# State stage of an S5 layer on one Trainium2 core: input products by column tiles, six rows' joins added by TensorE, table slots moved, two low parts later, first chunk behind four rows

## The chip, the cores and the metric

One core of one Trainium2 chip runs the whole kernel as one program. The metric is device time in microseconds (us), the median of several runs. Engines are named as in the profile: PE is TensorE (PEld its weight loads), DVE is VectorE, ACT is ScalarE, POOL is GpSimd, and SP is the queue that issues most DMAs. Each engine works through its own list in order and waits on semaphores.

## The reference

Two layers of a decoder over 256 tokens of width 2048. Layer 0 is attention; layer 1 is an S5 state-space layer with a GLU. Each layer ends with a LayerNorm, a SwiGLU feed-forward and another LayerNorm. The change lies in layer 1, in `_s5_glu`:

```python
u = h.astype(f32).reshape(B, S, S5_GROUPS, S5_GROUP)          # 128 groups of 16 channels
bu = jnp.einsum('bsgc,gpc->bsgp', u.astype(jnp.complex64), B_bar)
_, states = lax.associative_scan(combine, (a, bu), axis=1)    # 64 complex states a group
y = jnp.einsum('bsgp,gcp->bsgc', states, C_mat).real.reshape(B, S, D)
y = y + d_skip.astype(f32) * h.astype(f32)
z = jax.nn.gelu(y).astype(h.dtype)
val, gate = jnp.split(z @ w_glu, 2, axis=-1)
return val * jax.nn.sigmoid(gate)
```

## The kernel before

Most of the time goes to weight products. A weight matrix comes in chunks of 512 KB (two row tiles of 128 by 512 columns) into a ring of four `RAW` slots. ACT rounds a chunk to its high part (`hi`, L835), DVE subtracts to get the low part (`lo`, L1193), and PE multiplies high by high, low by high and high by low (L406 to L408): 12 matmuls a chunk. `load` (L282) issues the next chunk when `lo` has let go of its slot; semaphore `lo_ready` counts low parts.

The state stage stands between the last chunk of layer 0 and the GLU product. It works on 16 rows of 128 channels; a row has 512 state values (4 pairs of groups, real and imaginary, 64 slots of 4 tokens each).

1. **Input products** (L760). For a row, 8 matmuls with a 128 by 128 table `TS` as weights and 64 columns of `U4` as moving data fill one PSUM bank. ACT copies the bank to `ST` (L1121, semaphore `e_out`).
2. **Joins** (`join`, L1923). DVE turns slots into pairs of slots: `product` (L1905, coefficient times odd slots, 496 elements), `total` (L1910) and the sum with the even slots into the chain buffer `CH` (L1932). Two rows are interleaved. After 8 rows `join_fours` (L1958 to L1962) goes on to fours; then come 8 more rows and a second `join_fours`.
3. **Chain** (`chain_op`, L2002 to L2008): 14 serial steps over both halves on DVE.
4. **Going back down**: `fill_fours` (4 rows at a time), ACT's `even_states` (L1128) copies the even slots from `CH` into `ST`, and `grow` (DVE: L1905, L1910, L1946) fills the odd slots of a row.
5. **Local products** (L772): PE multiplies `UT` by the table `KTAB` in 32 by 32 tiles, into the banks that the outputs use. It waits for all 16 `e_out`.
6. **Read-outs** (`read_out`, L784): for a row 32 matmuls with 32-column weights from the row's second table and 64 columns of `ST`; the innermost loop goes over four groups of 32 PSUM partitions. Then ACT takes the gelu (L1137) of two rows at a time and its high part (L1145), and DVE the low part (`split_z`, L2030). GLU chunk `j` (`first_chunk`) needs rows 2j and 2j+1. `add_zeros` (L801) puts matmuls with a zero operand between.

A trace record of an fp32 matmul in L760, L784, L772 or L801 comes twice per matmul. SP loads the tables (16 input tables L311, 16 output tables L315) into 14 slots of 4 KB per partition, each when its slot is free, and after them the GLU chunks 4 to 7. `CH` lies in the first 16 KB, where the `RAW` ring is: the four low parts of GLU chunks 0 to 3 are made before it is written. The hand-written order on PE is:

```python
for row in range(5):
    add_zeros((26, 0, 4, 0, 8)[row])
    read_out(row)
add_zeros(6)
for j in range(per):
    first_chunk(j)
    for row in range(2 * j + 5, 2 * j + 7 if j < 4 else 2 * j + 8 if j == 4 else 0):
        read_out(row)
```

POOL loads the gains `GB` after the last input product and the input of the next small product (`p_tok`, L2332) after the last read-out; PE turns it (L450) right after GLU chunk 7.

Of the kernel before, what the change touches and what calls it, by code (L numbers as in the profile page):

```python
# [25 lines left out]
P = 128  # L26
# [3 lines left out]
KT = D // P  # L30
# [52 lines left out]
def build(nc, t, out):  # L83
# [3 lines left out]
    with ExitStack() as ctx:  # L87
# [54 lines left out]
        slot_kb = [160, 164, 48, 64, 52, 68, 56, 72, 60, 76, 168, 172, 176, 180]  # L142
# [46 lines left out]

        def tile_of(row):  # L190

            return row // 2 + KT // 2 * (row % 2)
# [39 lines left out]
        e_done, e_out, square, joined, grown, even_out = sem("e_done"), sem("e_out"), sem("square"), sem("joined"), sem("grown"), sem("even_out")  # L232
        fours_joined, fours_filled = sem("fours_joined"), sem("fours_filled")
# [34 lines left out]
        def _(sp):  # L268
# [40 lines left out]
            def input_table(row):  # L309

                sp.dma_start(TS[row % 14][:], e_dram[tile_of(row)].rearrange("p (a c n) -> p a c n", a=4, c=2)).then_inc(ts_in[row % 14], 16)  # L311

            def output_table(row):

                sp.dma_start(TS[row % 14][:], c_dram[tile_of(row)].rearrange("p (a c n) -> p a c n", a=4, c=2)).then_inc(ts_in[row % 14], 16)  # L315
# [6 lines left out]
            def out_with_tables():  # L322

                nb, per, c0, _ = PHASES["outB0"]
                for j in range(nb * per):
# [5 lines left out]
                    if j >= 8 and j % 4 == 0:  # L331
                        input_table(j // 4)
# [5 lines left out]
            def s5_loads():  # L338
# [9 lines left out]
                for row in (0, 1, 10, 11, 12, 13):  # L348
                    input_table(row)
                for row in (14, 15):  # L350
                    sp.wait_ge(e_done, row - 13)
                    input_table(row)
                for row in range(2, 14):
                    sp.wait_ge(e_done, row + 1)
                    output_table(row)
                for row in (0, 1):
                    sp.wait_ge(e_done, row + 15)
                    output_table(row)
                for row in (14, 15):
                    sp.wait_ge(y_done, row - 13)  # L360
                    output_table(row)
                sp.wait_ge(even_out, KT)
                for j in range(RING):
                    sp.wait_ge(y_done, 2 * j + 6)
                    glu_chunks(RING + j, RING + j + 1)
# [31 lines left out]
        def _(pe):  # L397
# [349 lines left out]
            for row in range(KT):  # L747
                pe.wait_ge(ts_in[row % 14], 16 if row < 14 else 32)
# [1675 lines left out]
```

## Time and profile before

| | us |
|---|---|
| median of 3 runs (2291.73 to 2292.98) | 2292.68 |
| the profiled execution's own time | 2296.42 |
| its span (first to last instruction) | 2294.6 |
| PE busy in the span | 2266.1 (99%) |
| DVE busy | 1679.3 (73%) |
| ACT busy | 1033.2 (45%) |

The span is that of the instructions, the time that of the whole execution. PE is busy almost everywhere; the places where it is not are few, and a share of busy time hides them. The state stage (about 1192 to 1310 us from the span's start) is read from the timelines of its engines.

### The profile page before, as it was taken

What the parts mean: (1) busy time and instruction counts of PE and PEld (TensorE: products, weight loads), DVE (VectorE), ACT (ScalarE), POOL (GpSimd) and SP (SyncE); (2) the same over time, 40 slices, a digit from 0 to 9 for tenths busy, and PEclk for the clock granted to TensorE, in tenths of its full rate; (3) what the DMA queues carried; (4) which work ended last, traced back from release to release, by engine and by line L of the source; (5) the groups of instructions that cost most, each with busy time, mean ns of one, the idle gap of its engine ahead of it and who ended that gap; (6) DMA issues with size and microseconds to landing.
All of it is one profiled execution on the core that took longest, in us unless ns stands there. A gap on an engine that the chain in (4) does not pass through costs nothing.

```text
span 2294.6 us, 34806 instructions
## 1 busy us (share of the span) xinstructions
PE 2266.1 (99%) x12036; PEld 1883.5 (82%) x12036; DVE 1679.3 (73%) x2539; ACT 1033.2 (45%) x1162; POOL 223.3 (10%) x322
## 2 busy tenths in 40 slices
PE   9999999999999999999999999999999999999998
PEld 7888888888887888888878788888888888888886
DVE  5775758778888878788879756766777654577666
ACT  4445636444444334444342544544455433444442
POOL 1000069701111111000100000000000000000000
PEclk9999999999999999999999999999999999999999
DMA  7655365778786777666765456665655666656664
GB/s 255 197 190 176 107 225 175 216 251 269 260 272 225 256 244 237 221 223 220 266 238 187 143 192 194 216 224 194 197 192 186 199 194 194 195 188 193 198 192 138
DMA packets 134619, 478.51 MB, mean 209 GB/s; under 512 B 15968, under 2 KB 19296, under 8 KB 133360
## 3 DMA queue, kind: packets, MB, share of 16 engines
q1 hardware_dynamic: 120720, 427.87, 56.8%
q0 software_dynamic: 13648, 49.12, 6.7%
q8 instruction: 71, 1.16, 0.2%
q14 instruction: 36, 0.29, 0.0%
q10 hardware_dynamic: 144, 0.07, 0.0%
HBM read 457.85 MB, written 19.14 MB: 208 GB/s over the span
## 4 chain that ended last, share of the span: by engine, by line
PE 94%; DVE 4%; ACT 1%; issue 1%; DMA 1%; DVEq 0%; ACTq 0%; SPq 0%
PE ps L406 29%; PE ps L408 29%; PE ps L407 29%; PE ps L760 1%; PE ps L450 1%; PE ps L784 1%; PE ps L420 0%; PE ps L422 0%; PE ps L421 0%; DVE w_lo L1193 0%; DVE gated L1607 0%; PE ps L675 0%; DMA raw<-in_w_outA 0%; DVE gated L1905 0%; DVE scan_wide L1958 0%
## 5 line engine op out<-in xcount | busy, mean ns | idle before, releaser
L1193 DVE TENSOR_TENSOR w_lo<-raw,w_hi 128x1024 fp32r<-128x1024 f32 x771 | 945.8, 1232 | 510.0 <-ACT w_hi L835 502.9
L835 ACT ACTIVATE w_hi<-raw 128x1024 fp32r<-128x1024 f32 x771 | 813.5, 1059 | 986.7 <-PE ps L408 863.0
L406 PE MATMUL ps<-w_hi,x_hi 128*128 128x512 f32 x2304 | 901.2, 391 | 2.0 <-DVE x_lo L2030 1.8
L408 PE MATMUL ps<-w_hi,x_lo 128*128 128x512 f32 x2304 | 897.5, 390 | 0.0
L407 PE MATMUL ps<-w_lo,x_hi 128*128 128x512 f32 x2304 | 897.3, 389 | 0.0
L406 PEld LDWEIGHTS ps<-w_hi,x_hi 128*128 128x128 f32 x2304 | 432.8, 188 | 92.1 <-issue 2.2
L408 PEld LDWEIGHTS ps<-w_hi,x_lo 128*128 128x128 f32 x2304 | 432.9, 188 | 90.8
L407 PEld LDWEIGHTS ps<-w_lo,x_hi 128*128 128x128 f32 x2304 | 433.0, 188 | 88.9
L406 PE MATMUL ps<-w_hi,hid_hi 128*128 128x512 f32 x656 | 256.8, 392 | 1.3 <-DVE w_lo L1193 1.3
L407 PE MATMUL ps<-w_lo,hid_hi 128*128 128x512 f32 x656 | 255.5, 389 | 0.0
L408 PE MATMUL ps<-w_hi,hid_lo 128*128 128x512 f32 x656 | 255.3, 389 | 0.0
L1607 DVE STREAM_TRANSPOSE gated<-gated 32x128 f32<-32x128 f32 x704 | 213.0, 303 | 9.8
L406 PEld LDWEIGHTS ps<-w_hi,hid_hi 128*128 128x128 f32 x656 | 123.1, 188 | 30.3 <-DVE w_lo L1193 3.1
L408 PEld LDWEIGHTS ps<-w_hi,hid_lo 128*128 128x128 f32 x656 | 123.1, 188 | 25.8
L407 PEld LDWEIGHTS ps<-w_lo,hid_hi 128*128 128x128 f32 x656 | 123.1, 188 | 25.2
L2143 POOL TENSOR_TENSOR s_small<-s_small 64x128 f32<-64x128 f32 x93 | 81.9, 881 | 7.5
L1049 ACT ACTIVATE hid_hi<-gated 128x512 f32 (+1 forms) x44 | 27.9, 633 | 120.7 <-DVE gated L1607 120.7
L2264 POOL DMA_DIRECT2D s_e_dram<-s_e x16 | 8.9, 556 | 335.6 <-DVE s_e L1687 335.6
L2113 POOL DMA_DIRECT2D gb<-in_ln_g x4 | 2.2, 544 | 397.6 <-DVE res L2063 128.6
L2257 POOL DMA_DIRECT2D s_coef<-s_coef_dram x64 | 35.4, 559 | 4.7 <-DMA s_coef_dram<-s_small 4.5
L1592 DVE TENSOR_TENSOR gated<-ps,gated 128x512 f32<-128x512 f32 x44 | 30.1, 685 | 5.7 <-ACT gated L1044 5.6
L1615 DVE TENSOR_TENSOR hid_lo<-gated,hid_hi 128x512 f32 (+1 forms) x44 | 30.1, 684 | 0.0
(306 smaller groups left out, 1431.0 us busy)
## 6 DMA issues: line engine op xcount, KB each, us to landing
raw<-in_w_inA SPq DMA_DIRECT2D x192, 512.0 KB, 4.2
raw<-in_w_inB SPq DMA_DIRECT2D x160, 512.0 KB, 4.2
raw<-in_w_outA SPq DMA_DIRECT2D x96, 512.0 KB, 4.2
raw<-in_w_outB SPq DMA_DIRECT2D x80, 512.0 KB, 4.2
raw<-in_w_in SPq DMA_DIRECT2D x64, 512.0 KB, 4.4
raw<-in_w_gate SPq DMA_DIRECT2D x64, 512.0 KB, 3.7
raw<-in_w_glu SPq DMA_DIRECT2D x64, 512.0 KB, 4.2
raw<-in_w_out SPq DMA_DIRECT2D x32, 512.0 KB, 3.4
```

Source lines behind the costliest of these rows:

```text
L406: pe.matmul(o, hi[:, kt + k, cols], WH[:, s, k, 0:width], start=(kt + k == 0), stop=False)
L407: pe.matmul(o, hi[:, kt + k, cols], WL[:, s, k, 0:width], start=False, stop=False)
L408: last = pe.matmul(o, lo[:, kt + k, cols], WH[:, s, k, 0:width], start=False, stop=(kt + k == depth - 1))
L450: last = pe.transpose(TP[:, g % 2, k, q * P:(q + 1) * P], src[:, q, col + k * P:col + (k + 1) * P], ID[:])
L835: act.activation(WH[:, s, :, 0:width], RAW[:, s, :, 0:width], ACT.Copy).then_inc(hi_ready, 1)
L1049: act.activation(HH[:, bass.ds(lin(2 * k, 2 * coef, i), 2), :], GT[:, 0], ACT.Copy).then_inc(hid_hi, 1)
L1193: dve.tensor_tensor(WL[:, s, :, 0:width], RAW[:, s, :, 0:width], WH[:, s, :, 0:width].bitcast(F32), ALU.subtract).then_inc(lo_ready, 1)
L1592: dve.tensor_tensor(GT[:, 1], A[:, bb % 2, :, 256:512], GT[:, 0], ALU.mult).then_inc(hid_ready, 1)
L1607: last = dve.transpose(turned_of[32 * j:32 * j + 32, :, :, r, :], rows_of[32 * r:32 * r + 32, :, :, j, :])
L1615: dve.tensor_tensor(HL[:, rows, :], GT[:, 0], HH[:, rows, :].bitcast(F32), ALU.subtract).then_inc(hid_split, 1)
L2143: link(pool.tensor_tensor(o, a, b, op))
L2257: pool.dma_start(EC[n][PW * s:PW * (s + 1)].rearrange("p a c n -> p a (c n)"), src).then_inc(e_raw[n], 16)
```

## The change

- **Input products.** Each matmul of 128-column weights is split into four with 32-column weights, one per group of 32 PSUM partitions, with the same moving data. `U4` is laid out with the row first.
- **Joins of rows 8 to 13.** DVE makes the product alone, into a buffer of the row's own (`SPREAD`). PE adds both its halves to the even slots of the row's PSUM bank, with the identity as weights (4 matmuls a row, 124 columns each, PSUM step 2), and ACT copies the even slots to `CH`. Rows 14 and 15 are joined as before, after the six products. Local products and the second `join_fours` wait for all six copies (`chain_out`).
- **Tables.** Rows 0 to 7 are loaded early (before: rows 2 to 9), and rows 14 and 15 take the slots of rows 8 and 9, behind five output tables.
- **Low parts.** Only those of GLU chunks 1 and 2 are made before the joins. The one of chunk 0 comes after the second `grow` pair, that of chunk 3 after the fifth. `CH` moves off their `RAW` slots, so chunk 4 can be loaded after `lo` of chunk 0, chunks 5 and 6 after 8 `even_states`, and chunk 7 after `lo` of chunk 3.
- **End of the stage.** PE reads out four rows, then does chunk 0, and from there two rows behind each of chunks 0 to 5. ACT takes gelu 0 and 1 ahead of the even states of rows 4 to 7. POOL's `GB` load waits for all even states.

```diff
-        CH = [at(f"chain{h}", [P, SLOTS // 2, PAIRS], 8 - 8 * h) for h in range(2)]
-        U4 = at("u_by_pair", [P, 4, KT, SLOTS], 96)
+        CH = [at(f"chain{h}", [P, SLOTS // 2, PAIRS], kb) for h, kb in enumerate((0, 100))]
+        U4 = at("u_by_pair", [P, KT, 4, SLOTS], 96)
+        SPREAD = [at(f"spread{n}", [P, 2, 2, 4, SLOTS // 2 - 1], kb) for n, kb in enumerate((96, 98, 202, 204, 108, 110))]
...
-                        last = pe.matmul(PS[:, row % 8, o:o + SLOTS], TS[row % 14][:, a, ri, :], U4[:, a, row, :], start=True, stop=True)
+                        for n_ in range(4):
+                            cols = slice(PW * n_, PW * (n_ + 1))
+                            last = pe.matmul(PS[cols, row % 8, o:o + SLOTS], TS[slot_of(row)][:, a, ri, cols], U4[:, row, a, :], start=True, stop=True)
                 last.then_inc(e_done, 1)
+            for row in range(8, 14):
+                pe.wait_ge(spread, row - 7)
+                for o in range(2):
+                    even = PS[:, row % 8, 4 * SLOTS * o:4 * SLOTS * (o + 1)].rearrange("p (a n) -> p a n", n=SLOTS)[:, :, 2:SLOTS:2]
+                    for c in range(2):
+                        last = pe.matmul(even, ID[:], SPREAD[row - 8][:, o, c], start=False, stop=(c == 1), skip_group_check=True)
+                last.then_inc(added, 1)
...
             pe.wait_ge(e_out, KT)
+            pe.wait_ge(chain_out, 6)
...
-            for row in range(5):
-                add_zeros((26, 0, 4, 0, 8)[row])
+            add_zeros(24)
+            for row in range(4):
                 read_out(row)
-            add_zeros(6)
+            add_zeros(10)
             for j in range(per):
                 first_chunk(j)
-                for row in range(2 * j + 5, 2 * j + 7 if j < 4 else 2 * j + 8 if j == 4 else 0):
-                    read_out(row)
+                if j < 6:
+                    read_out(2 * j + 4)
+                    read_out(2 * j + 5)
...
+            for row in range(8, 14):
+                act.wait_ge(added, row - 7)
+                first = 8 * (row % 8)
+                act.activation(CH[row // 8][:, 1:SLOTS // 2, first:first + 8].rearrange("p m x -> p x m"),
+                               PS[:, row % 8, :].rearrange("p (x n) -> p x n", n=SLOTS)[:, :, 2:SLOTS:2], ACT.Copy).then_inc(chain_out, 1)
...
-            for j in range(RING):
-                lo(PHASES["glu"][2] + j)
+            lo(PHASES["glu"][2] + 1)
+            lo(PHASES["glu"][2] + 2)
...
+            for row in range(8, 14):
+                dve.wait_ge(e_out, row + 1)
+                if row == 12:
+                    dve.wait_ge(e_done, KT)
+                product(row, slots_of(row, 1), SPREAD[row - 8]).then_inc(spread, 1)
+            for n_ in range(3):
+                join(14, n_)
+                join(15, n_)
+            dve.wait_ge(joined, 30)
+            dve.wait_ge(chain_out, 6)
+            join_fours(1)
...
-            pool.wait_ge(e_done, KT)
+            pool.wait_ge(even_out, KT)
             load_gb(1)
```

The first place is DVE's list at the second half of the joins: `spread` is a row's product for PE, `gated` the buffer of the usual join, `chain_93` the second half of `CH`. Before:

```order
L1962 TENSOR_TENSOR chain_92<-chain_92,scan_wide_115 128x15x8x4
L1905 TENSOR_TENSOR gated<-a_bar,states 128x496 x2
L1910 TENSOR_TENSOR gated<-gated 128x2x124 x2
L1932 TENSOR_TENSOR chain_93<-gated,states 128x8x31 x2
...
L1958 TENSOR_TENSOR scan_wide_114<-a_bar_111,chain_93 128x960
```

and now:

```order
L1998 TENSOR_TENSOR chain_92<-chain_92,scan_wide_121 128x15x8x4
L1941 TENSOR_TENSOR spread_95<-a_bar,states 128x496
...
L1941 TENSOR_TENSOR spread_100<-a_bar,states 128x496
L1941 TENSOR_TENSOR gated<-a_bar,states 128x496 x2
L1946 TENSOR_TENSOR gated<-gated 128x2x124 x2
L1968 TENSOR_TENSOR chain_93<-gated,states 128x8x31 x2
L1994 TENSOR_TENSOR scan_wide_120<-a_bar_117,chain_93 128x960
```

Four groups of six instructions became six single products and one such group.

The second place is PE's list from the last input product to the local products. Before:

```order
L760 MATMUL ps<-u_by_pair,s_table_97 128x64 x8
L760 MATMUL ps<-u_by_pair,s_table_98 128x64 x8
L772 MATMUL ps<-u,s_k 32x256 x4
```

and now:

```order
L773 MATMUL ps<-u_by_pair,s_table_111 32x64 x32
L773 MATMUL ps<-u_by_pair,s_table_112 32x64 x32
L780 MATMUL ps<-spread_95,ident 128x4x31 x4
...
L780 MATMUL ps<-spread_100,ident 128x4x31 x4
L793 MATMUL ps<-u,s_k 32x256 x4
```

A row has 32 matmuls in place of 8, and 24 additions that wait for DVE stand ahead of the local products.

The third place is DVE's list after the first `fill_fours`, where the low parts (`w_lo`, `x_lo`) stand between the rows, now:

```order
L1982 TENSOR_TENSOR states<-states,gated 128x8x31 x2
L1994 TENSOR_TENSOR scan_wide_120<-a_bar_117,chain_92 128x15x32
...
L1998 TENSOR_TENSOR chain_92<-chain_92,scan_wide_121 128x15x4x4
L2075 TENSOR_TENSOR x_lo<-z,x_hi 128x512
L1229 TENSOR_TENSOR w_lo<-raw,w_hi 128x1024
L1941 TENSOR_TENSOR gated<-a_bar,states 128x496 x2
```

Before, no low part of z and none of a weight stood between the second and the third pair of rows.

## Rows read from the trace of the kernel before
**Rows 1.** The page's first line: the whole execution.
```profile
span 2294.6 us, 34806 instructions
```
**Rows 2.** Busy time by stretch: length, PE, PEld, DVE, ACT, POOL; then PE's clock, DMA share, GB/s.
```profile
1231.30:1249.40 18.10, 17.79 (x513) 15.05 (x513) 18.03 (x78) 1.46 (x2) 0.73 (x2) 1.00 0.46 175
1255.40:1258.30 2.90, 0.01 (x1) 0.00 (x1) 2.32 (x6) 2.12 (x4) 0.00 (x0) 0.75 0.00 0
1258.30:1267.10 8.80, 8.77 (x260) 8.51 (x264) 5.23 (x13) 2.34 (x4) 0.00 (x0) 0.50 0.41 123
1273.90:1277.30 3.40, 3.40 (x10) 2.65 (x9) 3.37 (x10) 0.00 (x0) 0.00 (x0) 0.50 0.00 0
```
**Rows 3.** Timeline of PE: start us, us, line, operation, count, [idle before].
```profile
1196.20 1.86 PE L733 MATMUL ps<-ident,res 128*128 128x128 f32 x15 [0.20 <-DVE res L1459]
...
1201.83 28.80 PE L760 MATMUL ps<-u_by_pair,s_table 128*128 128x64 f32 x256
1231.31 7.69 PE L772 MATMUL ps<-u,s_k 32*32 32x256 f32 x215 [0.69 <-ACT states L1121]
...
1249.39 6.02 PE L801 MATMUL ps<-zeros,ident 128*128 128x64 f32 x52
1258.33 3.64 PE L784 MATMUL ps<-states,s_table 128*32 128x64 f32 x128 [2.92 <-DVE states L1946]
1261.90 1.97 PE L801 MATMUL ps<-zeros,ident 128*128 128x64 f32 x8
...
1277.72 1.99 PE L784 MATMUL ps<-states,s_table 128*32 128x64 f32 x128
...
1301.95 0.50 PE L406 MATMUL ps<-w_hi,x_hi 128*128 128x512 f32 x1
...
1310.26 0.60 PE L450 MATMUL ps<-ident,p_tok 128*128 128x128 f32 x4
```
**Rows 4.** Timeline of DVE, same columns.
```profile
1203.20 4.62 DVE L1193 TENSOR_TENSOR w_lo<-raw,w_hi 128x1024 fp32r<-128x1024 f32 x4
...
1217.07 0.68 DVE L1905 TENSOR_TENSOR gated<-a_bar,states 128x496 f32<-128x496 f32 x1 [0.48 <-ACT states L1121]
...
1219.37 2.23 DVE L1958 TENSOR_TENSOR scan_wide<-a_bar,chain 128x960 f32<-128x960 f32 x2
...
1223.90 1.26 DVE L1905 TENSOR_TENSOR gated<-a_bar,states 128x496 f32<-128x496 f32 x2
...
1234.82 2.23 DVE L1958 TENSOR_TENSOR scan_wide<-a_bar,chain 128x960 f32<-128x960 f32 x2
...
1239.36 0.49 DVE L2002 TENSOR_TENSOR scan_work<-a_bar,chain 128x128 f32<-128x128 f32 x2
...
1252.79 1.23 DVE L1958 TENSOR_TENSOR scan_wide<-a_bar,chain 128x480 f32<-128x480 f32 x2
...
1255.98 1.26 DVE L1905 TENSOR_TENSOR gated<-a_bar,states 128x496 f32<-128x496 f32 x2 [0.69 <-ACT states L1128]
...
1261.07 1.23 DVE L1958 TENSOR_TENSOR scan_wide<-a_bar,chain 128x480 f32<-128x480 f32 x2
...
1267.13 1.26 DVE L1905 TENSOR_TENSOR gated<-a_bar,states 128x496 f32<-128x496 f32 x2 [3.57 <-ACT states L1128]
```
**Rows 5.** Timeline of ACT, same columns.
```profile
1203.86 0.60 ACT L1121 ACTIVATE states<-ps 128x512 f32<-128x512 f32 x1 [0.73 <-PE ps L760]
...
1255.33 2.20 ACT L1128 ACTIVATE states<-chain 128x248 f32<-128x248 f32 x4 [22.55 <-DVE chain L1962]
...
1291.57 1.06 ACT L835 ACTIVATE w_hi<-raw 128x1024 fp32r<-128x1024 f32 x1 [3.80 <-DMA raw<-in_w_glu]
```
**Rows 6.** Instructions of the tile p_tok, with the time from issue to landing.
```profile
L2332 POOL DMA_DIRECT2D p_tok<-in_p x1: 734/734/734, 1302.3 to 1302.3; - x1
...
DMA to landing us min/median/max: 5.5/5.9/6.3
```
**Rows 7.** The same of the tables.
```profile
DMA to landing us min/median/max: 3.6/4.9/9.2
```

More of the change, by code:

```diff
@@ L188, in build, with slot_of @@
         c_dram = nc.dram_tensor("s5_c_dram", (KT, P, 4 * 2 * P), F32, kind="Internal").ap()
+        def slot_of(row):
+            return row if row < 14 else row - 6
         def tile_of(row):
@@ L747, in _ @@
             for row in range(KT):
-                pe.wait_ge(ts_in[row % 14], 16 if row < 14 else 32)
+                pe.wait_ge(ts_in[slot_of(row)], 16 if row < 14 else 32)
                 if row == 0:
@@ L776, in read_out @@
             def read_out(row):
-                pe.wait_ge(ts_in[row % 14], 32 if 2 <= row < 14 else 48 if row < 2 else 64)
+                pe.wait_ge(ts_in[slot_of(row)], 32 if row < 14 and row not in (8, 9) else 48 if row < 14 else 64)
                 pe.wait_ge(grown, 6 * (row // 2) + 5 + row % 2)
@@ L783, in read_out @@
                         for a in range(4):
-                            last = pe.matmul(outputs(row, a, s, s + 1), TS[row % 14][:, a, ri, PW * s:PW * (s + 1)],
+                            last = pe.matmul(outputs(row, a, s, s + 1), TS[slot_of(row)][:, a, ri, PW * s:PW * (s + 1)],
                                              ST[:, row, ri, a, :], start=False, stop=(ri == 1), skip_group_check=True)
@@ L1921, in join @@
             def join(row, n_):
-                done = 6 * (row // 2) + 2 * n_ + row % 2
+                done = 6 * (row // 2 if row < 8 else 4) + 2 * n_ + row % 2
                 if done >= 2:
@@ L1927, in join @@
                     dve.wait_ge(e_out, row + 1)
-                    ins = product(row, slots_of(row, 1))
+                    ins = product(row, slots_of(row, 1), wide[row % 2])
                 elif n_ == 1:
@@ L1941, in grow @@
                     dve.wait_ge(even_out, row + 1)
-                    ins = product(row, slots_of(row, 2))
+                    ins = product(row, slots_of(row, 2), wide[row % 2])
                 elif n_ == 1:
@@ L1980, in fill_fours @@
                         carry(4 * q, 4, n_, o, 2, 3).then_inc(fours_filled, 1)
-            dve.wait_ge(lo_ready, PHASES["glu"][2] + RING)
+            dve.wait_ge(lo_ready, PHASES["glu"][2] + 2)
             dve.wait_ge(square, 14)
-            for row in range(0, KT, 2):
+            for row in (0, 2, 4, 6):
                 for n_ in range(3):
@@ L1987, in _ @@
                     join(row + 1, n_)
-                if row % 8 == 6:
-                    dve.wait_ge(joined, 3 * (row + 2))
-                    join_fours(row // 8)
-                    dve.wait_ge(fours_joined, 6 * (row // 8 + 1))
+            dve.wait_ge(joined, 24)
+            join_fours(0)
+            dve.wait_ge(fours_joined, 6)
+            for row in range(8, 14):
+                dve.wait_ge(e_out, row + 1)
[8 more added lines that the diff above has]
+            join_fours(1)
+            dve.wait_ge(fours_joined, 12)
             def chain_op(h, n_, k):
@@ L2031, in split_z @@
                                   XH[:, rows, :].bitcast(F32).rearrange("p k n -> p (k n)"), ALU.subtract).then_inc(z_split, 1)
-            first = PHASES["glu"][2] + RING
+            first = PHASES["glu"][2]
             fill_fours(0)
-            for b in range(8):
+            grow_pair(0)
+            for b in range(1, 8):
                 grow_pair(b)
-                if b in (1, 2, 3):
+                if b > 1:
+                    split_z(b - 1)
+                if b < 4:
                     dve.wait_ge(grown, 6 * (b + 1))
@@ L2040, in _ @@
                     dve.wait_ge(fours_filled, 6 * (b + 1))
-                if 2 <= b < 6:
-                    split_z(b - 2)
-                if b == 6:
+                else:
+                    lo(first + b - 1)
+                if b == 1:
+                    split_z(0)
                     lo(first)
-                    split_z(4)
-            for b in range(5, 8):
-                lo(first + b - 4)
-                split_z(b)
+            lo(first + 7)
+            split_z(7)
             c0, b0 = PHASES["glu"][2:]
```

69 lines of the change are left out of this document (40 added, 29 removed).

## The prediction

> **What bounds the kernel now.** The span is 2294.6 us [rows 1], and outside the state stage PE runs without gaps, so only what moves the end of GLU chunk 7 moves the end of the kernel. I read the timelines of PE, DVE and ACT side by side through that stage, then the granted clock by stretch. From 1203.20 to about 1258 DVE has no gap to speak of: four low parts, the joins of rows 0 to 7 from 1207.85, `join_fours` at 1219.37, the second half's joins at 1223.90, `join_fours` at 1234.82, the chain at 1239.36, `fill_fours` at 1252.79, the first `grow` at 1255.98 [rows 4]. PE is behind it only once: row 7 comes 0.48 us late [rows 4]. PE's own work there (input products to 1230.6, local products from 1231.31 to 1249.39, zeros to 1255.4) ends early, and PE idles 2.92 us before the first read-out at 1258.33 [rows 3]. So the input products are not the bound, DVE's chain is.
>
> From 1258.33 the two alternate. In the idle time PE's clock falls from 2.4 to 1.2 GHz: mean 0.75 in that gap, 0.50 for the 8.8 us after it, and 0.50 again for 3.4 us under chunk 0 [rows 2]. At half clock two read-outs take 3.64 us against 1.99 at full [rows 3]. DVE waits 3.57 us at 1267.13 for even states that ACT holds back behind a high part and that behind a third read-out [rows 4], and ACT waits 3.80 us for a GLU chunk at 1291.57 [rows 5], since all chunk loads came after the last even state. Chunk 7 ends at 1310.26, where PE turns `p_tok` [rows 3].
>
> **Part 1, up to the second `join_fours`.** Two low parts less before the joins: 4.65 us for four [rows 4], so 2.33 less. The input products take 28.80 us for 16 rows, 1.79 each [rows 3]. The new ones have the form of a read-out (32 matmuls, 128 by 32 weights, 64 columns, four column groups innermost), which costs 0.96 us a row at full clock (1.99 us for two less the drain of the last) [rows 3]. So rows come at 0.96 us from 1201.83 and end near 1217.3. ACT's copy of 0.60 us [rows 5] keeps up, and row 7's wait (0.48) goes. Tables 14 and 15 are issued when rows 8 and 9 are done (1210.5 and 1211.5) behind five output tables. With a landing of 3.6 to 9.2 us [rows 7] row 15 may be up to 4.5 us late. Nothing needs it before DVE's fifth product at 1223.5, so I cost this at nothing.
>
> DVE then starts the joins at 1205.55, and the first `join_fours` ends 11.04 + 4.53 us later (from rows 4: 1219.37 less 1207.85 less 0.48, and 1223.90 less 1219.37), at T = 1221.1. Six products at 0.59 and one pair of joins (10.92 / 4 = 2.7) bring DVE to T + 6.3. PE cannot begin adding before the first product, at T + 0.7 = 1221.8. An addition is two records of a 128-wide identity; such a record costs 0.116 us with 64 zero columns (6.02 us for 52) and 0.12 in the token transposes (1.86 for 15) [rows 3]. Eight records a row are 0.9 us, six rows 5.4. But PE has then idled since about 1217.3, some 4.5 us, longer than the 2.92 us after which its clock stood at half [rows 2, 3]. The same record costs 0.24 at half clock (1.97 for 8) [rows 3], 1.8 us a row. Bounds for the end of the additions: 1227.2 at full clock, 1232.6 if all are at half. The half-clock stretches lasted 3.4 us under full chunks and 10.2 us from the gap on [rows 2], and the additions are dense, so I take a return after two to three rows, and an end at 1229.8. ACT's last copy and the hand-over add 0.9: J = 1230.7 (1228.2 to 1233.5) for the second `join_fours`, which stood at 1234.82. **Gain 4.1 us** (1.3 to 6.6).
>
> One rule speaks against this step. The identity's output has a PSUM step of two elements. The token transposes of L733 write with a far larger step (rearranged to `p q n s`) and cost 0.12 us a record, like the contiguous ones [rows 3]; I therefore charge nothing for the step. The Trainium skill (PSUM — Partial Sum Buffer, Specifications) says of PSUM that "any non-contiguous AP slows matmuls significantly". By that rule, with an estimate of twice the time, the sum would be 4 to 8 us less; it is rival C.
>
> **Part 2, chain and cover.** From `join_fours` to the first `grow` nothing changes: 1255.98 less 1234.82 = 21.16 us [rows 4], so `grow` starts at D = J + 21.2 = 1251.9 and row 0 can be read at D + 2.35 (1258.33 less 1255.98). PE's local products lose their head start: they too begin at J. They take 18.1 us and 24 zeros 5.5, so PE arrives at J + 23.6, and row 0 is ready at J + 23.5. The cover is used up to the last tenth, at no price, and the 2.92 us gap with its fall of the clock goes. What costs PE time after J now moves the end one for one.
>
> **Part 3, read-outs and chunks.** Times from D, with durations of [rows 3 to 5]: a pair of `grow` 2.55 (1261.07 less 1255.98, halved), `fill_fours` 2.54 (1255.33 less 1252.79), `split_z` 0.65, a low part 1.2, gelu 1.1, high part 0.55, two even states 1.1, a chunk 2.75 (8.31 us from 1301.95 to 1310.26 for three), two read-outs 1.92.
> - Rows 0, 1 from 2.35, rows 2, 3 from 4.9, zeros (2.3) to 9.1. DVE: `grow` 0 and 1, `fill_fours` 1 to 7.6, `split_z` 0 to 8.3, low part of chunk 0 to 9.5. Chunk 0 runs from 9.6 to 12.35. Even state 4 is there at 8.7 (gelu 1 starts at 7.0), so DVE no longer waits: the 3.57 us are gone, 1.85 of them refilled by the low parts.
> - Then DVE and PE keep step. `grow` 2 ends at 12.0, 3 at 17.7, 4 at 23.4, 5 at 27.7, 6 at 32.0, 7 at 36.3; chunks start at 14.3, 19.5, 25.3, 29.9, 34.6, 39.2 and 42.0. PE is short of work by 0.6, 1.0 and 0.2 us before rows 6, rows 8 and chunk 3.
> - Chunk 4 is issued at 9.6 and chunks 5 and 6 at 11, long before their high parts at 18, 24 and 27. Chunk 7 is issued at 25.4, needed at 31.7. The 3.80 us wait is gone.
> - Chunk 7 ends at D + 44.7. Before it was 1310.26 less 1255.98 = 54.3. **Gain 9.6 us.**
>
> New at the end: `p_tok` is issued after row 15, and now two chunks stand behind that row instead of three. Issue at D + 39.6 and 5.5 to 6.3 us to land [rows 6] give 45.1 to 45.9, against 44.7 for PE; the low part of chunk 8, behind `split_z` 7 and two norm steps of 1.2 us, ends at 45.3. **Loss 0.7 us.** `GB` now starts near D + 24 and is needed at D + 41.7: nothing. A clock that falls once more somewhere in part 3 costs half of a 3.4 us stretch, 1.7 us; PE has gaps of 1 us as the one before chunk 0, so I take 60% of it: **loss 1.0 us.**
>
> **Sum:** 4.1 + 9.6 − 0.7 − 1.0 = 12.0 us. Against the profiled execution (2296.42 us, a span of 2294.6 with 1.8 around it) that is 2284.4. The median of the runs is 3.74 lower, so I forecast 2292.68 − 12.0 = 2280.7 us.
>
> **Rivals.** No change means within 0.2% (4.6 us), about what a measurement of this kernel tells.
> - A, the clock never falls: J = 1228.2 and no loss in part 3, 2.5 + 1.0 more gain, 2277.2. For it: the local products hold 1.00 [rows 2]. Against it: 4.5 us without any matmul. Chance 0.12.
> - B, colder: additions all at half clock (2.8 later) and two more low stretches of 1.7, 2286.9. The 8.8 us at 0.50 under 32-column read-outs [rows 2] speak for it, as the stage is now richer in them. Chance 0.15.
> - C, strided additions twice as dear, by the rule above: J at 1234.7 to 1239, 4 to 8 us of the gain lost, 2284.7 to 2289. The row of L733 speaks against it. Chance 0.06.
> - D, the change doesn't do what it says: column tiles save nothing on the input products. They end at 1230.6, the additions at 1236.1, J = 1237.0, 6.3 later: 2287.0. The read-outs' 0.96 us speak against it. Chance 0.06.
> - E, slower: PE stays at half clock from the additions through the local products. These stood under the scan with 6 us of idle and zeros after them and now have no slack. Additions to 1232.6, J at 1233.5, 36.2 us of local products and 11 of zeros: row 0 at 1280.7 instead of 1254.3, 2280.7 + 26.4 = 2307. It decides once the low stretch eats 12 us, that is lasts some 24 us. I have no row of a rise under 32 by 32 tiles, only 1.00 throughout [rows 2]; but dense work raised the clock within 10.2 us. Chance 0.04.
>
> **Numbers.** The forecast has 0.57. The range reaches from A with a little more (2276.5) to B and the milder half of C and D (2287.5). Faster by over 0.2% (below 2288.1): forecast, A, nearly all of B and D, half of C, 0.88. Slower: E and a remainder, 0.05. Same: 0.07.
>
> **What would show it.** Input products at 0.96 us a row; DVE without a gap up to `join_fours`, then up to 4 us of waiting for ACT's last chain copy; additions at 0.9 or 1.8 us a row with the clock; row 0 with no gap before it and at full clock; chunk 0 9.6 us after the first `grow`; ACT never waiting for a GLU chunk; a wait of under 1 us at `p_tok`. Wrong if additions exceed 1.8 us a row, if the local products run at 0.50, or if chunk 7 ends later than 47 us after the first `grow`.

## The result and the profile after

The change makes the kernel **slower**: a median of 2301.68 us (2300.12 to 2303.34, 6 runs) against 2293.06 (2291.73 to 2294.49, 6 runs) before, a ratio of 1.0034 with a 95% interval of 1.0024 to 1.0044. The forecast was 2280.7, in a range of 2276.5 to 2287.5.

| | before | after |
|---|---|---|
| the profiled execution, us | 2296.42 | 2300.45 |
| its span | 2294.6 | 2298.7 |
| first input product | 1201.83 | 1201.72 |
| second `join_fours` (J) | 1234.82 | 1243.57 |
| first `grow` (D) | 1255.98 | 1264.74 |
| `p_tok` turned, behind GLU chunk 7 | 1310.26 | 1314.16 |
| from there to the end of the span | 984.3 | 984.5 |

In the two profiled executions all of the loss, and more, stands ahead of J: 8.75 us later, where 4.1 us earlier was forecast. Part 3 gives 4.9 back, against an execution of the kernel before that lies 3.4 us above its median. The timeline of PE after (columns as in [rows 3]) shows where it starts:

```profile
1201.72 1.53 PE L773 MATMUL ps<-u_by_pair,s_table 128*32 128x64 f32 x92
1204.13 1.99 PE L773 MATMUL ps<-u_by_pair,s_table 128*32 128x64 f32 x128 [0.88 <-issue]
1208.96 2.77 PE L773 MATMUL ps<-u_by_pair,s_table 128*32 128x64 f32 x127 [2.83 <-issue]
1212.96 3.64 PE L773 MATMUL ps<-u_by_pair,s_table 128*32 128x64 f32 x128 [1.23 <-issue]
1217.23 1.99 PE L773 MATMUL ps<-u_by_pair,s_table 128*32 128x64 f32 x127 [0.64 <-issue]
1221.07 1.99 PE L773 MATMUL ps<-u_by_pair,s_table 128*32 128x64 f32 x127 [1.84 <-issue]
1225.18 1.99 PE L773 MATMUL ps<-u_by_pair,s_table 128*32 128x64 f32 x127 [2.13 <-issue]
1232.60 4.71 PE L773 MATMUL ps<-u_by_pair,s_table 128*32 128x64 f32 x168 [5.43 <-issue]
1237.24 5.62 PE L780 MATMUL ps<-spread,ident 128*128 128x124 f32 x48
1243.62 17.59 PE L793 MATMUL ps<-u,s_k 32*32 32x256 f32 x512 [0.76 <-ACT chain L1149]
1261.14 5.57 PE L823 MATMUL ps<-zeros,ident 128*128 128x64 f32 x48
1267.09 1.99 PE L805 MATMUL ps<-states,s_table 128*32 128x64 f32 x128 [0.38 <-issue]
```

The products themselves run as forecast: 128 records, two rows, in 1.99 us. But after each 127 or 128 records PE stands idle, and the profile names "issue": it waited for no semaphore, no table, no engine. 128 matmul records with their 128 weight loads are 256 instructions. The DMA view of 1190 to 1245 us has a queue of kind "instruction" (packets, MB, share of 16 engines), before:

```profile
q8 instruction: 6, 0.10, 0.8%
```

and after:

```profile
q8 instruction: 9, 0.15, 1.1%
```

Packets of some 16 KB, three more of them in this window. Over the input products alone the same view counts 2 packets before (1201.7 to 1231.4) and 8 after (1201.7 to 1237.3). That is 512 and 2048 instructions in blocks of 256, and the whole span has 71 and 77. **PE's instructions are themselves loaded, 256 at a time, and the stretch now eats a block in 2 us while a new one comes every 4.2** (1204.13 to 1225.18 in five blocks). The Trainium skill (Runtime: NRT & Kernel Launch, Instruction fetch mechanics) describes such a refill in 16 KiB blocks of 256 instructions, and says that the cost of crossing a boundary is "mostly hidden"; the trace agrees with the block and not with the hiding. The longest gap, 5.43 us, stands behind 856 records, inside row 13, so it is not a wait for the tables of rows 14 and 15. DVE's waits in that time (timeline) are the consequence:

```profile
1210.46 0.68 DVE L1941 TENSOR_TENSOR gated<-a_bar,states 128x496 f32<-128x496 f32 x1 [1.64 <-ACT states L1144]
1214.99 0.68 DVE L1941 TENSOR_TENSOR gated<-a_bar,states 128x496 f32<-128x496 f32 x1 [1.78 <-ACT states L1144]
1218.73 0.68 DVE L1941 TENSOR_TENSOR gated<-a_bar,states 128x496 f32<-128x496 f32 x1 [0.99 <-ACT states L1144]
1237.43 1.26 DVE L1941 TENSOR_TENSOR spread<-a_bar,states 128x496 f32<-128x496 f32 x2 [9.43 <-PE ps L773]
1243.57 2.23 DVE L1994 TENSOR_TENSOR scan_wide<-a_bar,chain 128x960 f32<-128x960 f32 x2 [2.10 <-issue]
```

The last row but one are the products of rows 12 and 13, whose buffers lie on the part of `U4` that the last input products read: they wait 9.43 us for the last input product. By stretch (columns as in [rows 2]):

```profile
1201.70:1210.00 8.30, 4.59 (x304) 4.25 (x296) 6.88 (x11) 3.00 (x6) 0.00 (x0) 1.00 0.65 192
1210.00:1215.00 5.00, 3.77 (x147) 3.54 (x140) 2.76 (x7) 1.55 (x3) 0.00 (x0) 0.50 0.72 220
1237.20:1243.00 5.80, 5.66 (x53) 5.43 (x48) 4.03 (x8) 3.74 (x7) 0.00 (x0) 0.99 0.57 175
1243.00:1261.00 18.00, 17.38 (x512) 15.02 (x512) 17.40 (x88) 1.97 (x3) 0.00 (x0) 1.00 0.02 4
1264.00:1314.00 50.00, 44.97 (x1165) 37.46 (x1164) 42.80 (x84) 30.10 (x40) 1.84 (x3) 1.00 0.42 155
```

The clock stood at 0.50 from 1210 to 1215, after a stretch in which PE was idle for 3.7 of 8.3 us, and again under the last 168 products (4.71 us), after the gap of 5.43. It was at 1.00 under the local products and, as a mean, in all of part 3.

### The profile page after: what moved, and what is told of

Read it like the earlier page. It is cut to its first block, busy times and chain, and to the rows that moved or that the text cites. A ratio compares the mean times of both kernels' runs of the same rounds, so it can differ in the third digit from the quotient of the medians.

```text
span 2298.7 us, 36386 instructions
## 1 busy us (share of the span) xinstructions
PE 2255.7 (98%) x12832; PEld 1873.3 (81%) x12832; DVE 1674.2 (73%) x2527; ACT 1036.3 (45%) x1168; POOL 222.8 (10%) x322
## 4 chain that ended last, share of the span: by engine, by line
PE 94%; DVE 3%; issue 2%; DMA 1%; ACT 0%; POOL 0%; DVEq 0%; ACTq 0%; SPq 0%
PE ps L417 29%; PE ps L418 29%; PE ps L419 29%; PE ps L773 1%; PE ps L793 1%; PE ps L805 1%; PE ps L461 1%; DVE gated L1643 1%; DVE w_lo L1229 1%; PE ps L433 0%; PE ps L432 0%; PE ps L431 0%; DMA s_c_dram<-s_c_pow 0%; PE ps L823 0%; PE ps L686 0%
## 5 line engine op out<-in xcount | busy, mean ns | idle before, releaser
L773 PE MATMUL ps<-u_by_pair,s_table 128*32 128x64 f32 x1024 | 20.6, 252 | 15.0 <-issue 15.0
L1628 DVE TENSOR_TENSOR gated<-ps,gated 128x512 f32<-128x512 f32 x44 | 30.2, 686 | 4.6 <-ACT gated L1067 4.3
```

Source lines behind the costliest of these rows:

```text
L773: last = pe.matmul(PS[cols, row % 8, o:o + SLOTS], TS[slot_of(row)][:, a, ri, cols], U4[:, row, a, :], start=True, stop=True)
L1628: dve.tensor_tensor(GT[:, 1], A[:, bb % 2, :, 256:512], GT[:, 0], ALU.mult).then_inc(hid_ready, 1)
```

## The experiments

Theory F: the number of PE instructions, not their work, sets the end of the input products. F1 is its floor, a block at a time even on idle queues; F2 is contention, a block that comes late behind table transfers. J is given from the first input product, since that stood anywhere between 1200.3 and 1204.2 us from run to run; in the kernel before it is 33.0 us, after the change 41.9. Each ratio is against the kernel before, on the same chip. Medians of two runs can come from two chips, and then the ratios are the better comparison.

### Wide input products in the changed kernel

```diff
-                        for n_ in range(4):
-                            cols = slice(PW * n_, PW * (n_ + 1))
-                            last = pe.matmul(PS[cols, row % 8, o:o + SLOTS], TS[slot_of(row)][:, a, ri, cols], ...)
+                        last = pe.matmul(PS[:, row % 8, o:o + SLOTS], TS[slot_of(row)][:, a, ri, :], ...)
```

> Input products back to 8 matmuls of 128-wide weights a row, the rest as changed. Theory F (PE's instruction blocks of 16 KB come too slowly for 32 matmuls a row: the rows of the changed kernel show a gap after every 127 or 128 records): a row takes 1.79 us again without gaps, input products end at 1230.6, additions at about 1236.1, second join_fours at 1237.0 instead of 1243.6, so 6.5 us less than the changed kernel, near 2295. Rival T (tables 14 and 15 come late, the 5.43 us gap at 1227.2 is a wait for them): the gap stays, join_fours at 1240 or later, 0 to 3 us less. Rival K (the fall of PE's clock is what costs): no more than 2 us less.

Measured: 2294.34 us, ratio 1.0002 (0.9992 to 1.0012): 7.3 us less than the changed kernel, and no difference from the kernel before. PE's timeline has no gap:

```profile
1204.21 28.80 PE L771 MATMUL ps<-u_by_pair,s_table 128*128 128x64 f32 x256
1232.84 5.57 PE L778 MATMUL ps<-spread,ident 128*128 128x124 f32 x48
```

J is at 34.9 us (1239.12). The late tables were held to be worth 3 us at most and the clock 2, so neither explains it. It is the column tiles that made the change slower. The rest of it, with wide products, is worth nothing in the median.

### Column tiles alone in the kernel before

```diff
-                        last = pe.matmul(PS[:, row % 8, o:o + SLOTS], TS[row % 14][:, a, ri, :], ...)
+                        for n_ in range(4):
+                            cols = slice(PW * n_, PW * (n_ + 1))
+                            last = pe.matmul(PS[cols, row % 8, o:o + SLOTS], TS[row % 14][:, a, ri, cols], ...)
```

> The kernel before with nothing changed but the input products by 32-column tiles. Theory F: gaps after every 128 records, products end near 1232 to 1237 as in the changed kernel, joins of rows 12 to 15 wait for them; slower than before by 2 to 8 us. If column tiles did what the prediction took them to do (0.96 us a row) it is 0.5 us faster than before.

Measured: 2296.75 us, ratio 1.0016 (1.0006 to 1.0026). The same gaps stand between the blocks, 0.61, 2.83, 1.51, 1.19, 2.12, 2.40 and 1.14 us, and the products end near 1234.0. So the gaps don't need the rest of the change. J is at 35.6 us (1237.07), 2.7 later than before, where the changed kernel had it at 41.9: there the additions stand behind the late products. This profiled execution (2294.1) lies 2.7 us under the median of its runs. In it PE reached row 0 with a gap of only 0.28 us and kept its clock at 1.00 from there to the turn of `p_tok`, which was thus 1.8 us sooner behind the first input product than in the trace of before. So it doesn't show where the median loses its 3 us.

### Output tables out of the way

```diff
-                for row in range(5):
-                    sp.wait_ge(e_done, row + 1)
-                    output_table(row)
                 for row in (14, 15):
                     sp.wait_ge(e_done, row - 5)
                     input_table(row)
+                sp.wait_ge(e_done, KT)
+                for row in range(5):
+                    sp.wait_ge(e_done, row + 1)
+                    output_table(row)
```

> The changed kernel with the output tables issued only after the last input product; input tables 14 and 15 as before. It tells two forms of theory F apart. F1 (blocks have a floor of about 3.8 us each even with idle DMA queues, since the next one is asked for only when the last is begun): input products still take about 30 us and end near 1231. F2 (blocks are late because table loads fill the DMA queues): gaps shrink to under 0.5 us, input products end near 1219 to 1221, second join_fours near 1229 to 1231 and the kernel is 12 us faster than the changed one, near 2290. Rival T: input products end near 1219 too, but with the only gap before row 14.

Measured: 2298.6 us, ratio 1.0022 (1.0011 to 1.0032). PE's timeline is now regular:

```profile
1205.52 1.99 PE L774 MATMUL ps<-u_by_pair,s_table 128*32 128x64 f32 x128 [1.92 <-issue]
1208.98 1.99 PE L774 MATMUL ps<-u_by_pair,s_table 128*32 128x64 f32 x127 [1.46 <-issue]
...
1224.10 1.99 PE L774 MATMUL ps<-u_by_pair,s_table 128*32 128x64 f32 x127 [2.12 <-issue]
1227.95 1.99 PE L774 MATMUL ps<-u_by_pair,s_table 128*32 128x64 f32 x127 [1.86 <-issue]
...
1232.51 5.62 PE L781 MATMUL ps<-spread,ident 128*128 128x124 f32 x48
```

From 1205.52 to 1227.95 six blocks take 3.74 us each as a mean, on queues that are all but empty in the first of these stretches:

```profile
1204.00:1215.00 11.00, 5.97 (x383) 5.50 (x384) 8.79 (x17) 3.58 (x6) 0.00 (x0) 1.00 0.02 5
1215.00:1233.00 18.00, 9.15 (x553) 8.41 (x553) 11.46 (x21) 5.14 (x9) 0.00 (x0) 1.00 0.21 63
```

Blocks at a DMA share of 0.02 or less took 3.46 to 3.86 us, and two at 0.28 and 0.62 took 3.83 and 4.11. That is the floor of F1; the reason that F1 gives for it was not tested. F2 is what the output tables add: the products end 30.4 us after the first one instead of 35.5, and the gap of 5.43 is gone. J is at 36.8 us (1238.85) instead of 41.9. Of the 20 us between the forecast end of the products (1217.3) and the measured one, some 15 are the floor and some 5 contention, with the half clock that followed the long gap. The transfers that were moved then fell on the local products, whose blocks came late by 0.53 and 1.65 us.

### Two 64-column tiles instead of four of 32

```diff
-                        for n_ in range(4):
-                            cols = slice(PW * n_, PW * (n_ + 1))
+                        for n_ in range(2):
+                            cols = slice(2 * PW * n_, 2 * PW * (n_ + 1))
```

> The changed kernel with two 64-column tiles instead of four of 32: 16 matmuls a row, half the instructions of the changed kernel, twice those of before. Theory F with a block every 3.8 to 4.3 us: 64 instructions a row, a block lasts 4 rows, so 1.0 to 1.1 us a row; input products end near 1219, additions start as DVE gives them, join_fours near 1229 to 1231, 12 us faster than the changed kernel, near 2290. If narrow tiles were slow in themselves: no better than 1.79 us a row. Rival T: a gap of some 5 us before row 14 stays.

Measured: 2287.67 us, ratio 0.9975 (0.9965 to 0.9984): **faster than the kernel before**. PE's timeline:

```profile
1200.47 6.63 PE L773 MATMUL ps<-u_by_pair,s_table 128*64 128x64 f32 x219
1208.24 3.95 PE L773 MATMUL ps<-u_by_pair,s_table 128*64 128x64 f32 x127 [1.14 <-issue]
1213.33 3.94 PE L773 MATMUL ps<-u_by_pair,s_table 128*64 128x64 f32 x126 [1.14 <-issue]
1220.06 1.99 PE L773 MATMUL ps<-u_by_pair,s_table 128*64 128x64 f32 x40 [2.79 <-issue]
1221.98 6.58 PE L780 MATMUL ps<-spread,ident 128*128 128x124 f32 x48
```

A row costs 32 records of 0.031 us, 0.99 us, as much as 64 records of 0.0155 us with four tiles. The second halving saves nothing on PE and doubles the instructions. A block lasts 3.95 us here, just over the floor of 3.46 to 3.86. J is at 28.8 us (1229.27).

### Without PE's additions, wide and with half tiles

```diff
-            for row in range(8, 14):
-                pe.wait_ge(spread, row - 7)
...
-                product(row, slots_of(row, 1), SPREAD[row - 8]).then_inc(spread, 1)
...
+            for row in (8, 10, 12, 14):
+                for n_ in range(3):
+                    join(row, n_)
+                    join(row + 1, n_)
```

> The changed kernel with the input products back at 128 columns and without TensorE's additions: rows 8 to 15 are joined by DVE as before. What is left of the change is the low parts, the slots of the tables and the new order of read-outs, chunks and transfers. Theory F (only the number of PE instructions went against the change): J is set by the 28.8 us of wide products plus the last pair of joins, some 2.7 us sooner against the start of the products than with wide products and additions (34.9 us there), so about 32.2 us; the end is 2.7 us before that run, 2291.5. Rival (the additions do help even with wide products): not faster than 2294.3.

> 64-column tiles, and rows 8 to 15 joined by DVE instead of six of them added on PE. DVE alone sets the second join_fours: joins of the first half 11.0, join_fours 4.5, joins of the second half 10.9 from 1204.24 give J = 1230.7 against 1229.27 with the additions, so 1.4 us later, 2289.1. If the additions are worth what the prediction held, which had DVE out of work for up to 4 us, it is 4 us later (2291.5); if PE's extra 96 records and the instruction block that they need cost more than they give, it is faster than 2287.7.

Measured: 2294.22 us for the wide one, ratio 0.9999 (0.9990 to 1.0008), and 2291.8 with half tiles, 0.9989 (0.9980 to 0.9998). J came at 33.0 us (1234.47) and 30.2 us (1231.19), 1.9 us before and 1.4 us behind the runs with additions. The first should have gained 2.7 us against the run with additions and gained nothing; the second should have lost 1.4 and lost 4.1 by the medians, 3.2 by the ratios. Neither theory had the cause. Without additions the local products start early again and PE is idle ahead of row 0, for 3.95 and 7.70 us. With half tiles (PE's timeline, then the two stretches):

```profile
1254.70 6.07 PE L797 MATMUL ps<-states,s_table 128*32 128x64 f32 x256 [7.70 <-DVE states L1969]
```

```profile
1247.00:1254.70 7.70, 0.00 (x1) 0.04 (x2) 6.90 (x26) 2.20 (x4) 0.00 (x0) 0.65 0.00 0
1254.70:1260.70 6.00, 6.00 (x257) 5.91 (x257) 5.60 (x14) 1.77 (x2) 0.00 (x0) 0.60 0.02 5
```

Four rows take 6.07 us at a clock of 0.60, against 5.04 with two block gaps in the run with half tiles and additions (1252.77 to 1257.81). From row 0 to the turn of `p_tok` 50.3 and 50.0 us pass, against 48.0 and 46.6 with additions. So a part of what the additions give seems to be that they hold back PE's cover until it ends beside row 0. It is not the whole of it: both runs without additions also have a longer gap in the read-out of rows 10 and 11 (3.27 and 2.60 us, "issue"), with clocks of 0.85 and 0.72 beside it. No run divides the two.

### Fewer zeros

```diff
-            add_zeros(24)
+            add_zeros(12)
```

> 64-column tiles and 12 zeros instead of 24 behind the local products, nothing else. PE reaches the read-outs 2.8 us before row 0. If the idle time costs the clock, as before the change, where 2.92 us without work were followed by 8.8 us at 0.50, the first four rows take twice as long and the kernel is 1.5 to 3 us slower than with half tiles alone (2289 to 2291). If it doesn't, the time stays at 2287.7, and the zeros are not needed.

Measured: 2289.59 us, ratio 0.9981 (0.9972 to 0.9990), 1.9 us more than half tiles alone, on another chip; the intervals of the two ratios overlap. PE idles 3.03 us ahead of row 0, and four rows again take 6.07 us, as expected of the clock. Row 0 to the turn of `p_tok` is 49.0 us, 2.4 more than in the profile of half tiles alone. Four slow rows took 1 us more than there; behind them stands a second fall of the clock (0.66 in the stretch from 15 to 20 us behind row 0). Between the two this run doesn't divide the loss.

### GB later

```diff
             pool.wait_ge(even_out, KT)
+            pool.wait_ge(hi_ready, PHASES["glu"][2] + RING + 4)
             load_gb(1)
```

> 64-column tiles, and the two transfers of GB are issued only after the high part of GLU chunk 7 (some 10 us later). Theory G (GB takes the bandwidth that chunk 7 and the last tables need, and this reaches PE): ACT's wait of 5.2 us for chunk 7 falls under 2 us, PE's gaps between chunk 5 and chunk 6 (0.47 and 0.49) shrink, and the kernel is up to 1 us faster, 2286.7. Rival (PE has work all the time, so that wait costs nothing): ACT's wait shrinks and the turn of p_tok stands no earlier against row 0; GB, issued near 1287 and 8 to 12 us in landing, is then late for the norm at 1295.8, and the kernel is the same to 2 us slower.

Measured: 2288.47 us, ratio 0.9975 (0.9966 to 0.9984), as without this edit. ACT's wait for chunk 7 (5.05 us in the changed kernel, 5.21 with half tiles) is gone altogether; in its place DVE waits 1.44 us for `GB` and PE 1.02 us for `p_tok`. The rival is borne out in the time: the kernel is no faster. That the wait itself cost nothing isn't shown, since the later `GB` brought PE's wait of 1.02 us with it.

### Four rows added instead of six

```diff
-            for row in range(8, 14):
+            for row in range(8, 12):
                 pe.wait_ge(spread, row - 7)
...
+            for row in (12, 14):
+                for n_ in range(3):
+                    join(row, n_)
+                    join(row + 1, n_)
```

> 64-column tiles, and only rows 8 to 11 added by PE; DVE joins rows 12 to 15, which fills the 3.07 us that it waited for the additions. If the rest of that wait is PE's (products until 1222.0, six rows of additions 6.6): four rows end near 1226.4 and DVE's own work at 1219.8 + 2.4 + 5.4 = 1227.6, J 1.6 us earlier, 2286.0. If what limits J is something else (the last copy of ACT, the landing of tables 14 and 15), J stays at 1229.3 and the time at 2287.7.

Measured: 2287.64 us, ratio 0.9969 (0.9958 to 0.9981), J at 28.6 us (1229.35) where 1.6 us less than 28.8 was expected. PE's timeline says why:

```profile
1220.89 2.40 PE L773 MATMUL ps<-u_by_pair,s_table 128*64 128x64 f32 x40 [3.89 <-issue]
1223.22 5.42 PE L780 MATMUL ps<-spread,ident 128*128 128x124 f32 x32
```

The last block of products came 3.89 us late, and the additions behind it cost 0.17 us a record at a clock of 0.69, where with six rows they cost 0.14 at 0.85. Two rows less on PE were eaten by that.

### Half tiles with quiet tables, with six and with four rows

Output tables after the last input product and 12 zeros, in the kernel with half tiles; the second has four rows added as well.

> 64-column tiles, the output tables issued only after the last input product, and 12 zeros instead of 24 behind the local products (2.8 us less, as room for gaps there). Theory F2 (the long gap of 2.8 to 3.9 us before the last block of the input products is an instruction block that comes late because table transfers fill the DMA queues): that gap falls to 1.5 us or less, the products end 1.5 to 2.5 us sooner, J is at most 27.5 us after the first product instead of 28.8, and the kernel is 1 us faster than with half tiles alone, 2286.5. If a block takes its time with idle queues too, or if the moved transfers then hold up the blocks of the local products by more than the 2.8 us of room, it is at 2287.7 or later.

> 64-column tiles, four rows added by PE and four joined by DVE, the output tables after the last input product, 12 zeros. With the late block out of the way PE ends four rows of additions near 25 us after the first product, and DVE's own work (27.1 us after it) sets J: 1.7 us before half tiles alone, 2286.0, if theory F2 of the run with quiet tables holds. If J follows the blocks all the same, J stays at 28.5 us after the first product and the time at 2287.6.

Measured: 2286.73 us, ratio 0.9970 (0.9957 to 0.9982), and 2286.94, 0.9974 (0.9964 to 0.9983). The gap before the last block shrinks to 1.73 and 0.80 us, and with idle queues up to 472 records run without a gap. PE's timeline with six rows:

```profile
1205.41 11.30 PE L774 MATMUL ps<-u_by_pair,s_table 128*64 128x64 f32 x380 [0.56 <-issue]
1218.44 1.91 PE L774 MATMUL ps<-u_by_pair,s_table 128*64 128x64 f32 x40 [1.73 <-issue]
1222.04 7.78 PE L781 MATMUL ps<-spread,ident 128*128 128x124 f32 x48 [1.69 <-DVE spread L1942]
```

The products end 18.4 us after the first instead of 21.5, but J stays at 28.6: PE is now early, waits 1.69 us for DVE, and its additions take 7.78 us at a clock of 0.71. F2 holds for the gap; of the 3.1 us that the products gained, half is left when DVE's product is there, and the rest is given back at the lower clock. The first read-outs were cold here as well: after 1.65 us without work 256 records took 5.44 us at 0.70. With four rows PE waits 3.89 us for DVE and 32 additions take 6.42 us at 0.57. DVE's own work then sets J, at 27.2 us (1227.46) as expected, but row 0 to the turn of `p_tok` took 48.9 us instead of 46.6.

### The same with 19 zeros

> 64-column tiles, four rows added by PE, the output tables after the last input product, and 19 zeros, which reach to row 0 within 0.5 us where 12 left PE idle for 1.96 us. If that idle time is what made part 3 of the run with 12 zeros 2.3 us longer (row 0 to the turn of p_tok 48.9 us, against 46.6 with half tiles alone), it is 46.6 us again, and with J at 27.2 us after the first product the kernel comes to 2285.3. If part 3 stays at 48 to 49 us, the loss comes from the instruction blocks and tables around chunk 0, and the time stays at 2286.9.

Measured: **2285.55 us**, ratio 0.9966 (0.9954 to 0.9979). PE's timeline:

```profile
1249.89 4.46 PE L824 MATMUL ps<-zeros,ident 128*128 128x64 f32 x38
1254.59 1.99 PE L806 MATMUL ps<-states,s_table 128*32 128x64 f32 x128 [0.24 <-issue]
...
1301.58 0.66 PE L462 MATMUL ps<-ident,p_tok 128*128 128x128 f32 x4
```

J is at 27.2 us again, and row 0 to `p_tok` is 47.0 us, near the 46.6 expected. That seems to bear out the idle time as the cause, but the stretches say otherwise. With 12 zeros:

```profile
1260.97:1265.97 5.00, 2.87 (x132) 2.23 (x130) 4.97 (x13) 0.00 (x0) 0.00 (x0) 1.00 0.61 214
1265.97:1270.97 5.00, 5.00 (x49) 3.79 (x48) 3.46 (x9) 4.84 (x7) 0.00 (x0) 0.66 0.01 3
```

Its first four rows ran at full clock behind the 1.96 us of idle time. What it lost it lost 15 us behind row 0, after the gap of 2.13 us in the read-out of rows 4 and 5. All runs with this order and additions have such a gap; the fall after it only some:

| run | row 0 to `p_tok`, us | gap in rows 4 and 5 | clock 15 to 20 us behind row 0 |
|---|---|---|---|
| changed kernel | 47.1 | 1.74 | 1.00 |
| half tiles | 46.6 | 2.23 | 1.00 |
| wide inputs | 48.0 | 2.00 | 0.66 |
| half, GB later | 48.0 (1.02 of it `p_tok`) | 2.28 | 0.66 |
| half, 12 zeros | 49.0 | 2.58 | 0.66 |
| four tiles, quiet | 47.7 (0.50 of it `p_tok`) | 2.44 | 1.00 |
| half, four rows added | 47.1 | 1.20 | 1.00 |
| half, quiet, 12 zeros | 46.7 | 1.28 | 1.00 |
| half, four, quiet, 12 zeros | 48.9 | 2.13 | 0.66 |
| half, four, quiet, 19 zeros | 47.0 | 2.30 | 1.00 |

After a gap of 2.0 to 2.6 us there the clock fell in four profiles of seven. Those four took 48.0 to 49.0 us (one of them with 1.02 of waiting for `p_tok`), and all others 46.6 to 47.7. Half tiles with quiet tables and 12 zeros had slow first rows and no fall there, and took 46.7: so slow first rows alone need not cost anything. Whether the zeros ahead of row 0 have a part in the later fall is open; it was not tried apart from them. This version has the lowest median of all. Its interval overlaps that of half tiles alone, so that it beats those is not shown; that both beat the kernel before is.

## Why the prediction was wrong

- **The step that failed** is in part 1: "So rows come at 0.96 us from 1201.83 and end near 1217.3." The price of a row was right where PE ran. What failed was to carry a price read from 128 records over to 1024 in a row, with nothing in the sum for the supply of the instructions themselves. The products ended at 1237.3, 20 us later. In the trace of before, 32-column tiles only come in stretches of up to 256 records, between chunks (12 records in 2.75 us) and zeros, or at half clock, where a block lasts 3.64 us [rows 3]; a new block had time to arrive. The sign was there all the same, in PE's timeline of that trace: `1300.80 1.23 PE L784 MATMUL ps<-states,s_table 128*32 128x64 f32 x71 [0.73 <-issue]`. Over 8 blocks in a row the floor is about 3.7 us a block. 2048 instructions took 30.4 us even without the output tables beside them, more than the 28.80 of the wide products.
- **Rival D** (the column tiles save nothing) came nearest in its place, with 0.06, but it held 2287.0, since it let the products end at 1230.6 and the additions go well. They ended 6.7 us later than that, some 5 of them contention, and J came 6.6 us after its 1237.0. Against the profiled execution 3 us more are those of part 3, which the rival took from the forecast. The rival on the slower side (E, half clock under the local products) did not happen: 1.00 there.
- **Additions**: 48 records in 5.62 us at full clock, 0.117 each, as forecast at the lower bound. I had put them at half clock for two to three rows after 4.5 us without work; there was no such pause, because the products were late. The half tiles with quiet tables made one, and there the fear came true: after waits of 1.69, 3.89 and 3.21 us a record of the additions cost 0.16, 0.20 and 0.17 us, at clocks of 0.71, 0.57 and 0.69. The PSUM step of two costs nothing here, with 124 columns; rival C fell. (A record of zeros with 64 columns takes as long, 0.116, so the columns are not what sets the time, and a dearer write could hide behind it.) The rule of the Trainium skill behind it (PSUM — Partial Sum Buffer, Specifications: "any non-contiguous AP slows matmuls significantly") is not borne out by these records.
- **Sum of part 1**: J at 1243.57 against 1230.7, 12.9 us later.
- **Part 2** was right: D is J + 21.17 (forecast 21.16), the local products took 17.59 us (18.1), row 0 came at D + 2.35, and the gap of 2.92 us became 0.38.
- **Part 3** was 3.0 us short: `p_tok` was turned at D + 49.4, forecast 44.7 + 0.7 + 1.0 = 46.4, before 54.3. The loss of clock was not there in this profile (in several of the experiments it was). PE had six gaps ended by "issue" from row 0 on, 0.38, 0.49, 0.55, 1.74, 0.63 and 1.22 us, 5.0 in all. That these make up the 3.0 us was not tried alone.
- **The 4.9 us that part 3 did gain are hardly the new order's.** In the profile of column tiles alone the old order of read-outs and chunks ran at a clock of 1.00 throughout and took 49.8 us (D = 1258.24, `p_tok` at 1308.03), 0.4 more than the new one. So the old order does not need 54.3. What stands above 49.8 most likely goes with the cold read-outs behind the gap of 2.92 us, though these are single profiles. The medians agree: with wide products J is 1.9 us later than before and the kernel 0.6 us slower, within 2.3, so all that stands behind J gave back some 1.3 us; the forecast had 9.6 − 0.7 − 1.0 = 7.9. This term was mis-sized too.
- **GB: "nothing"** was right for the time and wrong for the trace. It held up chunk 7 on ACT by 5.05 us, and taking a like wait away made the kernel no faster. `p_tok` made PE wait 0.20 us.

In the sum: −12.0 forecast, 12.9 lost ahead of J, 3.0 in part 3 and 0.2 behind it give +4.1 us; the two profiled executions differ by 4.03. The medians differ by 8.6. The profiled execution before lies 3.4 above its median and the one after 1.2 below, which is the difference; where an execution of before spends 3.4 us more than another no second trace of it shows. An estimate: outside the stretch from the first input product to `p_tok` the 14 profiled executions spend 2186.3 to 2190.4 us (time less that stretch), and the one of before spends 2188.0. So its 3.4 us more likely lie in the state stage, in the cold read-outs that part 3 was measured against.

## What to carry to other kernels

An instruction has a price of its own on TensorE that shows only in a long row of short ones: count the instructions of a stretch, weight loads too, divide by 256, and compare the time of such a block with what the trace shows for its "instruction" queue (here 3.5 to 3.9 us on idle queues, 4.2 and more beside other transfers). When a matmul is split to save time, take the coarsest split that reaches the rate. And where work is moved off PE or made faster, look at what it does next: PE's idle times of 1.65, 2.92, 3.03, 3.95 and 7.70 us ahead of the read-outs were each followed by a lower clock (means of 0.50 to 0.72 under the first rows), and one of 1.96 us was not. And check what the profiled execution stands for before a gain is read from it: this one lay 3.4 us above its median, and the time that the change was to win back was largely a clock that another run of the old order didn't lose.

## What was unexpected of the hardware

- PE's gaps after every 127 or 128 records, of 0.4 to 5.4 us, with nothing waited for; one block of 256 instructions per 3.46 to 3.86 us at a DMA share of 0.02 or less.
- A block that comes late beside table transfers at a share near 1.00: the gap before the last block was 2.5 to 3.9 us in the five runs with half tiles and early tables, and 0.8 to 1.7 once the transfers were moved.
- 64-column tiles reach the rate of 32-column ones: 0.031 us a record for twice the columns, against 0.1125 for 128.
- At a mean clock of 0.60 256 read-out records ran without a gap (6.07 us), where at full clock they took 5.04 with gaps. The supply of instructions takes away a part of what the clock gives.
- Of seven profiles with a gap of 2.0 to 2.6 us in the read-out of rows 4 and 5, four had the clock at 0.66 in the stretch from 15 to 20 us behind row 0 and three had it at 1.00.
